# Moving the second half of the front's chunk recurrence and the samples' turn into the expert phase

## The reference, cut to what matters

```python
h = rmsnorm(x); p = h @ w_in                       # 3072 columns
y_conv = conv_mixer(...)                           # 256 channels, width 31
y_rwkv = rwkv_mixer(...)                           # 6 heads of 64: the recurrence below
y_att = sb_attention(...)                          # 6 heads; samples also read 1024 cached positions
x = x + concat(y_conv, y_rwkv, y_att) @ w_out
x = x + peer(rmsnorm(x))                           # 8 heads x 16 experts of 16384 per position

def _wkv_step(S, inp):                             # one position, every head, S is 64x64
    r, w, k, v, kk, b = inp
    sa = einsum('bhvk,bhk->bhv', S, kk)
    S = S * w[:, :, None, :] - sa[..., None] * b[:, :, None, :] + v[..., None] * k[:, :, None, :]
    return S, einsum('bhvk,bhk->bhv', S, r)
# then per head: (y - mean) * rsqrt(var + eps) * g + b, plus a bonus, times a gate
```

## Time and profile before

| | us |
|---|---|
| median of 3 runs | 3682.92 (3682.07 to 3686.68) |
| the profiled execution | 3688.43 |
| its span, first to last instruction | 3686.6 |

### The profile page before, as it was taken

The page is one execution under the profiler, slowest core; times in us unless marked ns, Lnnn a source line. Parts: engine busy times, 40 slices in busy tenths (PEclk is TensorE's granted clock), DMA queues, the critical chain, the costliest instruction groups (busy, mean ns, idle before and its releaser), DMA issues.

```text
span 3686.6 us, 52803 instructions
## 1 busy us (share of the span) xinstructions
PE 2809.8 (76%) x19164; PEld 1377.4 (37%) x19164; DVE 2585.6 (70%) x6424; ACT 1461.0 (40%) x2994; POOL 1383.0 (38%) x1205
## 2 busy tenths in 40 slices
PE   8999867667667876877688777777777777766656
PEld 4555465433224432443244334333433332323211
DVE  2477233577877787778777877788778876777775
ACT  2222112343723373338333843385338632223222
POOL 0000000144445345544454455445444555454443
PEclk9999997889888887898888888988898888778879
DMA  3112404599999999999999999999999999999998
GB/s 96 36 54 85 149 3 149 219 370 405 394 406 412 385 385 406 414 405 391 406 411 408 388 388 414 406 384 411 406 404 377 399 415 415 404 414 412 414 417 336
DMA packets 248118, 1252.97 MB, mean 340 GB/s; under 512 B 57577, under 2 KB 84497, under 8 KB 112177
## 3 DMA queue, kind: packets, MB, share of 16 engines
q0 software_dynamic: 160256, 1132.54, 76.0%
q1 hardware_dynamic: 87600, 117.05, 9.2%
HBM read 1226.61 MB, written 22.89 MB: 339 GB/s over the span
## 4 chain that ended last, share of the span: by engine, by line
PE 26%; DMA 21%; DVE 18%; ACT 10%; issue 7%; POOL 1%; another core or an unknown queue 0%; DVEq 0%; SPq 0%; ACTq 0%; POOLq 0%
PE peer_y L2289 14%; DMA uv_first<-in_peer_uv,expert 10%; DMA uv_rows<-in_peer_uv,expert 10%; PE peer_s L1977 4%; DVE uv_first L1754 4%; DVE uv_rows L1754 3%; PE scan L2082 2%; ACT L1944 2%; PE beside L2008 2%; ACT diag L1952 2%; ACT L1892 2%; DMA w_out_rows<-in_w_out 1%; DVE same L1457 1%; DVE same L1459 1%; DVE pick L1461 1%
## 5 line engine op out<-in xcount | busy, mean ns | idle before, releaser
L1413 POOL DMA_INDIRECT uv_first<-in_peer_uv,expert x604 | 706.7, 1170 | 1071.8 <-PE peer_y L2289 780.0
L2289 PE MATMUL peer_y<-uv_first,diag 64*64 64x512 f32 x4688 | 743.8, 748 | 402.4 <-ACT diag L1952 367.3
L1754 DVE CUSTOM_DVE_ANT_0 uv_first<-uv_first,p_h 128x1024 f32<-128x1024 f32 x604 | 728.4, 1223 | 198.6 <-DMA uv_first<-in_peer_uv,expert 185.9
L2289 PE MATMUL peer_y<-uv_rows,diag 64*64 64x512 f32 x3504 | 561.0, 750 | 297.8 <-ACT diag L1952 281.2
L1413 POOL DMA_INDIRECT uv_rows<-in_peer_uv,expert x452 | 533.2, 1180 | 659.5 <-PE peer_y L2289 577.0
L1754 DVE CUSTOM_DVE_ANT_0 uv_rows<-uv_rows,p_h 128x1024 f32<-128x1024 f32 x452 | 545.9, 1223 | 138.8 <-DMA uv_rows<-in_peer_uv,expert 136.8
L1944 ACT ACTIVATE gelu<-hidden 128x2 f32<-128x2 f32 x528 | 107.8, 204 | 1109.8 <-DVE hidden L1754 1054.9
L1952 ACT ACTIVATE diag<-p_ident,weights 128x128 f32<-128x128 f32 x1024 | 355.8, 395 | 478.9 <-DVE weights L1481 435.8
L2289 PEld LDWEIGHTS peer_y<-uv_first,diag 64*64 64x64 f32 x4688 | 181.7, 158 | 764.3 <-ACT diag L1952 512.4
L2289 PEld LDWEIGHTS peer_y<-uv_rows,diag 64*64 64x64 f32 x3504 | 134.9, 157 | 563.1 <-ACT diag L1952 396.2
L591 PE MATMUL proj<-mix,w_in_tile 128*128 128x512 f32 x672 | 296.9, 600 | 0.0
(11 more groups left out here) (413 smaller groups left out, 4162.4 us busy)
## 6 DMA issues: line engine op xcount, KB each, us to landing
w_out_rows<-in_w_out SPq DMA_DIRECT2D x50, 512.0 KB
w_in_tile<-in_w_in SPq DMA_DIRECT2D x24, 512.0 KB, 3.3
uv_first<-in_peer_uv,expert POOLq DMA_INDIRECT x604
uv_first<-in_w_query SPq DMA_DIRECT2D x8, 1024.0 KB, 6.7
uv_rows<-in_peer_uv,expert POOLq DMA_INDIRECT x452
pages_ring<-scratch_k_tiles SPq DMA_DIRECT2D x36, 192.0 KB
pages_ring<-out_v_new SPq DMA_DIRECT2D x36, 192.0 KB
scan_in<-scratch_scan_in SPq DMA_DIRECT2D x12, 480.0 KB
```

Of the source, the lines that this page charges most:

```text
L1413: pool.indirect_dma_start(out=uv(m, ALL, slice(0, 2 * D)), out_offset=None, in_=io["peer_uv"], in_offset=bass.IndirectOffsetOnAxis(ap=expe ...
L1754: nc.vector.tensor_tensor_reduce(out=uv(m, ALL, slice(0, D)), in0=uv(m, ALL, slice(0, D)), in1=h2[:, b % 2, :], scale=1.0, scalar=0.0, op0 ...
L2289: ins = nc.tensor.matmul(Y[r][rows[j], :], diag[rows[r], m % (2 * GP), rows[r]], uv(m, rows[r], slice(D + j * 512, D + (j + 1) * 512)), st ...
```

## The change

Only block 0's two chunks stay in `scan_rwkv` (one turn), which no longer loads the samples' state and masks. `finish_rwkv` handles block 0 alone, all three pairs in one instruction, and leaves its result in `mixed_first`; gates 1 and 2 follow the first six key products. Chunk 0 of block 1 runs in `peer`'s prelude, its steps 0 to 8 in beats 2 to 10 of block 0's attention and 9 to 15 between the parts of closing, scores and choice; the last key products move from beat 3 to beat 2, and the first output product from 3 to 4. In the expert phase block 0 holds chunk 1 of block 1 (from beat 1) and both of block 2 (from 25 and 43), with finishes from 18 and 59. Blocks 1 to 5 keep their steps. Block 6 holds the samples' turn in 26 steps from beat 35, with the state in the place of `w_out` rows, and block 7 its finish in beats 0 to 4. Finished rows stay in SBUF, in two buffers, where the closing reads them; the round by `mixed` goes. The helpers `scored`, `kept`, `chosen`, `exped` and `gated` give the same places as the lines that they replace. The diff is cut; the steps of `scan_sample` are those of the samples' turn before, cut into beats.

```diff
-FRONT = 2
+FRONT = 1
 NCH = SEQ // CH
 CPB = P // CH
+LATER = NBLK - 1 - FRONT
...
                         for slot, rows in ((2 * p, sb.kq[:, p, :]), (2 * p + 1, tile(R0 + p)), (2 * PR + p, tile(K0 + p)),
                                            (3 * PR + p, sb.bh[:, p, :]), (4 * PR + p, tile(V0 + p))):
                             sp.dma_start(io["scan_in"][:, :, slot, :].rearrange("n p c -> p n c"),
                                          rows[:, later].rearrange("p (n c) -> p n c", c=CH)).then_inc(scan_out, 16)
-                        sp.dma_start(io["finish_in"][:, :, 0, p, :].rearrange("b p n -> p b n"),
-                                     tile(p)[:, later].rearrange("p (b n) -> p b n", n=P)).then_inc(scan_out, 16)
+                        sp.dma_start(io["finish_in"][0:LATER, :, 0, p, :].rearrange("b p n -> p b n"),
+                                     tile(p)[:, FRONT * P:SEQ].rearrange("p (b n) -> p b n", n=P)).then_inc(scan_out, 16)
+                        sp.dma_start(io["finish_in"][LATER][:, 0, p, 0:CH], tile(p)[:, SEQ:SC]).then_inc(scan_out, 16)
                 if i == TILES:
                     sp.wait_ge(evicted, NT)
...
-        s0, tmask = t("state_sample", [P, PR, DB, HD]), t("seq_mask", [P, DB, HD])
-        spread, w0, values_by_seq = t("spread", [P, DB, HD]), t("w_state", [P, PR, HD]), t("values_spread", [P, DB, HD])
...
         pieces = [(0, 512), (512, 512), (1024, SC - 1024)]
         EARLY = FRONT * P
-        done = [(0, 0, EARLY), (EARLY, SEQ, SC - SEQ)]
...
+            load_queries(sp, io, sb, SLOTS + PR)
+            sp.wait_ge(V.sem, V.at("gated"))
+            sp.dma_start(io["mixed_first"], out[:, :, :]).then_inc(mix_out, 16)
             load_queries(sp, io, sb, SLOTS + PR + 1)
-            sp.wait_ge(mix_out, 16 * (PR + 1))
...
+            sp.wait_ge(mix_out, 16)
+            sp.wait_ge(g_out, 16 * 2 * PR)
...
-    scanned = lambda b: b + FRONT if b + FRONT < ATTENDED else None
+    scans = lambda b: ((1, 1, 1, 1), (2, 0, 25, 1), (2, 1, 43, 1)) if b == 0 else \
+        ((b + 2, 0, 2, 1), (b + 2, 1, 20, 1)) if b + 2 < ATTENDED else ()
+    finishes = lambda b: ((1, 18), (2, 59)) if b == 0 else ((b + 2, 36),) if b + 2 < ATTENDED else ((ATTENDED, 0),) if b == S_TURN + 1 else ()
+    S_STEPS = 26
...
+                for step in range(rate * (n - first), rate * (n - first) + rate):
+                    if step in range(16):
+                        scan(block, c, step)
+            if b == S_TURN and n - S_SCAN in range(S_STEPS):
+                scan_sample(n - S_SCAN)
+            for block, first in finishes(b):
+                if n - first in range(5):
+                    finish(block, n - first)
             if b == 0:
...
-        CLOSED = {3: range(0, 1), 5: range(1, 3), 6: range(3, 4), 8: range(4, 5)}
+        AHEAD = {1: range(24, 28), 2: range(28, 32)}
+        CLOSED = {4: range(0, 1), 5: range(1, 3), 6: range(3, 4), 8: range(4, 5)}
+        BESIDE = 2
...
-                    if b >= FRONT:
-                        sp.wait_ge(mixed_out, 16 * (b - FRONT + 1))
                     sp.dma_start(mixb[:, :, :], io["mixed"][b]).then_inc(mix_in, 16)
...
+            def scan_load_sample():
+
+                sp.wait_ge(FV.sem, FV.at("gated", LATER - 1))
+                sp.dma_start(xin[:, :, :], io["scan_in"][LATER * CPB]).then_inc(state_in, 16)
+                sp.dma_start(smask[:, :, :], io["scan_masks_sample"]).then_inc(state_in, 16)
+
...
+            scan_load(1, 0)
+            sp.dma_start(smask[:, :, :], io["scan_masks"]).then_inc(close_in, 16)
+            sp.dma_start(ident[:, :], io["ident"]).then_inc(close_in, 16)
+            sp.dma_start(gain2[:, :], io["norm2_g"]).then_inc(close_in, 16)
             begin_close(0)
+            sp.dma_start(ykept[:, 0, :, :], io["mixed_first"]).then_inc(first_in, 16)
             weights(0, 0)
             weights(0, 1)
-            sp.dma_start(gain2[:, :], io["norm2_g"]).then_inc(close_in, 16)
-            sp.dma_start(ident[:, :], io["ident"]).then_inc(close_in, 16)
...
-            sp.dma_start(smask[:, :, :], io["scan_masks"]).then_inc(const_in, 16)
...
+                        scan_load(1, 1)
+                        scan_load(1, CPB)
+                        scan_load(2, 0)
+                    elif scans(b):
+                        scan_load(b + 2, 1)
+                    if b == S_TURN:
+                        scan_load_sample()
                     for c in range(2, DC - 1):
                         weights(b + 1, c)
-                if scanned(b) is not None:
-                    scan_load(scanned(b), CPB)
-                if late_att(b) is not None:
-                    attention(late_att(b))
-                if scanned(b) is not None:
-                    sp.wait_ge(FV.sem, FV.at("gated", b))
-                    sp.dma_start(io["mixed"][scanned(b)][:, CT:CT + PR, :], ykept[:, :, :]).then_inc(mixed_out, 16)
+                if b == 0:
+                    attention(2)
+                    scan_load(2, 1)
+                    scan_load(2, CPB)
+                elif scans(b):
+                    scan_load(b + 2, CPB)
+                    if late_att(b) is not None:
+                        attention(late_att(b))
+                if b == S_TURN:
+                    sp.wait_ge(wo_used, ATTENDED * DC)
+                    sp.dma_start(s0, io["state_wkv"]).then_inc(state_in, 16)
+                    sp.wait_ge(ACT_S.sem, ACT_S.at("y"))
+                    sp.wait_ge(PE_S.sem, PE_S.at(f"out{PR - 1}"))
+                    sp.dma_start(fin[:, :, :, 0:CH], io["finish_in"][LATER][:, :, :, 0:CH]).then_inc(xin_in, 16)
+                    sp.wait_ge(DVE_S.sem, DVE_S.at(f"out{PR - 1}"))
+                    sp.dma_start(io["wkv_new_sample"], s0).then_inc(state_out, 16)
+                    sp.wait_ge(state_out, 16)
             sp.wait_ge(XV.sem, XV.at("state", chunk_at(ATTENDED - 1, CPB - 1)))
...
-                    if c == 0 and b > FRONT:
-                        act.wait_ge(mixed_out, 16 * (b - FRONT))
-                    keep_step("y", ykept[:, :, c * CH:(c + 1) * CH], r1_of(1))
+                    if c == 0:
+                        act.wait_ge(wo_used, (b - 1) * DC)
...
                     key_kept(nc, act, None, sb, Y, k)
                 attend(0, n)
+                if n >= BESIDE:
+                    scan(1, 0, n - BESIDE)
+            scan(1, 0, 9)
             close_root(0)
+            scan(1, 0, 10)
+            scan(1, 0, 11)
+            scan(1, 0, 12)
             close_turned(0)
             act.wait_ge(const_in, 16 * 9)
             keep(0)
+            scan(1, 0, 13)
             keep(1)
+            scan(1, 0, 14)
             exps(0)
+            scan(1, 0, 15)
             exps(1)
...
-                left = mixb[:, c, :] if c < DC - PA else att[:, c - (DC - PA), :]
+                if c == CT:
+                    if b:
+                        pe.wait_ge(FV.sem, FV.at("gated", b - FRONT))
+                    else:
+                        pe.wait_ge(first_in, 16)
+                recurrent = s_mixed if last(b) else ykept[:, b % 2, :, :]
+                left = mixb[:, c, :] if c < CT else recurrent[:, c - CT, :] if c < CT + PR else att[:, c - (CT + PR), :]
                 if b and c == DC - 1:
...
+                if m in range(PR):
+                    if m == 0:
+                        pe.wait_ge(state_in, 16 * 3)
+                        pe.wait_ge(FV.sem, FV.at("centre", LATER - 1))
+                        pe.wait_ge(FA.sem, FA.at("root", LATER - 1))
+                    if m == 2:
+                        kept_by_dve("spread0")
+                    for r in rows:
+                        ins = mm(RB[m % 2][r, :], kr[r, 2 * m, :], s0[r, m, :, :])
+                    PE_S.did(ins, f"in{m}")
+                if m == 4:
...
+                            ins = nc.tensor.matmul(lo(1)[r, i, q], s0[r, i, b, :], kr[r, 2 * i + 1, q], start=False, stop=True, skip_group_check=True)
+                    PE_S.did(ins, "y")
+                if m in (20, 22, 24):
+                    i = (m - 20) // 2
+                    kept_by_dve(f"spread_u{i}")
+                    if i == 1:
+                        kept_by_act("y")
+                    if i == 2:
+                        kept_by_dve("add0")
+                    for r in rows:
+                        mm(RB[i % 2][r, :], vk[r, PR + i, :], values[r, :, :], stop=False)
+                        ins = mm(RB[i % 2][r, :], bt[r, i, :], spread[r, :, :], start=False)
+                    PE_S.did(ins, f"out{i}")
+
...
 
-                k = b - FRONT
+                k, n_col = b - FRONT, CH if b == ATTENDED else P
+                by_row = lambda bank: bank[:, 0:PR * n_col].rearrange("p (i n) -> p i n", n=n_col)
                 if n == 0:
-                    pe.wait_ge(XA.sem, XA.at("y", chunk_at(b, CPB - 1)))
-                    pe.wait_ge(XV.sem, XV.at("state", chunk_at(b, CPB - 1)))
...
                 close_y(0, c)
```

(7 more changed lines are left out.)

869 lines of the change are left out of this document (480 added, 389 removed).

## The result

| | before | after |
|---|---|---|
| median of 4 runs, us | 3684.8 (3682.07 to 3696.96) | 3646.6 (3642.56 to 3655.36) |
| ratio, 95% interval | | 0.9892 (0.9869 to 0.9915) |
| profiled execution, us | 3688.4 | 3650.5 |
| its span, us | 3686.6 | 3648.7 |
| first expert gather, us | 698.65 | 609.19 |

The kernel is faster, by 31 to 48 us as the interval has it. The forecast was 3610 us in a range of 3590 to 3636, and the time lies above the range. In what follows, before is the kernel before the change and after the changed one. The profile of after says where the gain stayed: the front gave 89.5 us, 86.6 were forecast; the expert phase grew by 51.6 us, 14.1 were forecast.

A forecast was written before the change was run, and what follows sets the result against it. A front bound by chains between compute engines, then an expert phase bound by DMA transfers. Profiled 3688.4, less 86.6 for the earlier first gather, plus 14.1 in the expert phase, is 3615.9; less 5.5, 3610 us (range 3590 to 3636).

The forecast's parts named there:

- Projection, +1.9: Front, projection: longer stores on SyncE's queue delay the last w_in load; +1.9 us, bounds 0 and +3.
- Constants, turn 1, samples' turn, barrier, -98.5: Front, recurrence: fewer constant loads -3.2, turn 1 gone -34.8, samples' turn gone -61.0, a remaining barrier +0.5 us.
- Group norm's stage, 37 to 38 us: Front, group norm, gate and key products: 43.8 us shrinks to 37 to 38, so -6; bounds -9 and +1.
- Prelude, +16: Front, before the first expert gather: sixteen steps of one added chunk lengthen the 72.3 us by 16; bounds 0 and 29.
- Step 10's wait for zt: Prelude: step 10 waits for ScalarE's zt behind the closing's square and root, delaying the gain broadcast; +3 us.
- the rival with the prelude at its lone price: Prelude: the chunk costs what it takes alone, +29 us instead of 16; 3623 us in all, chance 0.12.
- Bytes, +3.1: Expert phase: net +1.2 MB of transfers costs +3.1 us at 400 GB/s; the state load lands in some 4 us.
- Block 0, +4 with bounds of 0 and +10: Expert block 0: one more chunk and finish, 12.8 us of TensorE and 6 of VectorE, lengthen it by 4 us.
- Block 6, +7 with bounds of 0 and +25: Expert block 6: the samples' turn, 38 us of TensorE over 26 beats, partly covered, lengthens it by 7 us.
- TensorE becomes the bound where work was put: Rival: blocks 0 and 6 cost their upper bounds, +25 + 10 instead of 11; 3634 us, chance 0.14.
- Its sign, TensorE over 90% busy there: Block 6, beats 35 to 60: TensorE expected over 90% busy and the transfer rate below 400 GB/s.
- The slower rival: Rival, expert phase: each of 52 new steps lengthens its beat; at 1.9 us a step 3698 us; chance 0.04.

The follow-up runs named there:

- the four edits: Changed kernel plus two chunks per expert block, y step over three beats, two beats from state product to use, recurrence steps before scores on TensorE: 3619.2 us, 0.9817.

## Why the prediction was wrong

Its base was the median of 3682.9; in the profile its misses are -2.9 us in the front and +37.5 in the expert phase, and the profiled execution stood 3.9 above the median, not 5.5.

- **Projection, +1.9: measured +4.6.** The load issues at 384.36, where 384.3 was worked out from the stores of the earlier trace rows. But the bound of 3 was wrong: TensorE idled 3.26 us instead of 0.54 for it, and some 1.7 us more came up by the stage's end; their cause is open.

```profile
381.40 2.25 SPq L228 DMA_DIRECT2D scratch_finish_in<-prc  x1
383.70 0.61 SPq L230 DMA_DIRECT2D scratch_finish_in<-prc  x1
384.36 1.24 SPq L206 DMA_DIRECT2D w_in_tile<-in_w_in  x1
```
```profile
389.69 3.10 PE L611 MATMUL proj<-w_in_tile,mix 128*128 128x384 f32 x6 [3.26 <-DMA w_in_tile<-in_w_in]
```

- **Constants, turn 1, samples' turn, barrier, -98.5: measured -99.4** (137.97 us of the earlier trace rows against 38.55). Right; VectorE's first copy comes 3.6 us earlier in the stage, where 3.2 were put.
- **Group norm's stage, 37 to 38 us: 35.6.** Right in kind, 2 us too careful.
- **Prelude, +16: +13.6.** The sum is right, its parts are partly luck. Up to the row that answers to 656.61 (558.66 in after) +2 was put and 5.1 measured, from there to the end of the closing products +10 and 3.6, behind them +5.4 and 4.8 (the three add up to 17.4; 16 was taken). So the closing products end 8.7 us later after the prelude's begin, where 10 to 14 were named. Step 10's wait for zt behind square and root was there, longer than thought (4.45 us at 582.52). The gather at 609.2 lies in the stated 600 to 622; the rival with the prelude at its lone price is out.
- **Bytes, +3.1.** The state load issued at 3016.87 us and landed 8.7 us later, twice the 4 that were worked out, but still inside its three beats. By the run without the turn's compute, block 6 keeps 4 us and block 7 3 for the turn's bytes and its finish, and blocks 1 to 5 hold 5 to 6 us together that no experiment touched; that may be bytes or chance. Blocks 1 to 5 each stayed within 4 us, two of them outside the 3 that I had named, about the scatter. (In the earlier trace rows the sixth slice is at 0 and the eighth at 5, not full as I wrote; nothing in the sum hangs on it.)
- **Block 0, +4 with bounds of 0 and +10: +12 to +21.** The failed step. It compared averages, "12.8 us of TensorE, 6 of VectorE, on 244 and 274 busy of 352". The room that counts is what VectorE waits for gathers: 30 us over the block in the kernel before, but 4.9 in beats 45 to 60, where attention 2 runs and where the chunk was put. And the chunk takes from it not its 4 us of VectorE alone, but also its waits for TensorE (6.2 us). The sum also put nothing for the start of block 1's second chunk in beat 1, behind the third scores (a wait of 6.4 us); by beat 9 block 0 is 5 to 7 us behind.
- **Block 6, +7 with bounds of 0 and +25: +25.** The second failed step. The size lies at the upper bound, but not for the bound's reason. The step weighed TensorE's load, "107 + 38 = 145 of 144 us". That load never came: TensorE's busy time in beats 35 to 63 rose from 115.4 to 134.8 us of 178.8, as the granted clock rose from 0.78 to 0.83, and with the four edits to 126.7 of 155.5 us, with no loss in that stretch. The step named one heavy step (10.5 us; 7.9 in after) and left out VectorE, which gets 16.1 us of work there and 31.7 us of waits for TensorE, 47.8 us. Its waits for gathers, 34.2 us, went down to 7.7 and gave 26.5 of that; with 2.0 us of waits for gelu and other gaps the stretch is 23.3 us longer.
- **The rivals.** "TensorE becomes the bound where work was put", 3634 us, came nearest in time and place, and its mechanism is refuted by the runs with two beats from product to use, with steps ahead of the scores and with the four edits: the same matmuls, 14, 7 and 16 us less in block 6 (12, 5 and 15 with block 7). Its sign, TensorE over 90% busy there, didn't come either: 75%. The slower rival had the right loop, but its uniform price is refuted by the run with two chunks in every block. What I called for it, POOL's wait on peer_y, doesn't tell waits of the loop from those of full rings; VectorE's waits do.

The 96 small matmuls of beat 53 took 7.9 us, 82 ns each, after 109 in the earlier trace rows. The difference is the clock: in after they start 56 ns apart up to 3148.4 us, at a granted clock of 0.99, and 104 ns apart from 3149.9 us on, at 0.50; in the earlier trace rows the granted clock is 0.56. The Trainium skill ("TensorE: Matmul & The Clock Gate", section "Wait — 56ns, not 53.3ns?") has 25 ns as the least distance of two small matmuls; neither row comes near it, and the rows were rightly preferred, though the sum hardly hung on it: without them, block 6 lost 2.5 us less.

The 5 to 7 us of beats 0 to 9 in block 0 are placed (a step behind the scores) but not settled in size. With two beats from product to use, block 6 is still 11 us behind before, 8.9 of them in beats 35 to 63; there they went only with the three other edits in place, so the y step's share is not shown apart.

## What to carry to other kernels

When work is put beside a saturated transfer, don't compare its length with an engine's idle share of a stage. Read from the stretch itself how long the engine that consumes the transfers waits for them; in the two stretches read here that was the most that could be taken, and the added work draws on it with its busy time on that engine and with every wait for another engine that it brings into that engine's order. A step that is handed to another engine and read back one beat later makes a serial round with everything queued ahead of it there: leave two beats, keep it out of beats with a long item ahead of it, or put it ahead of that item. Where the consumer still waits for transfers, as in the kernel before, such a round cost nothing that could be measured.

## What the runs showed of the hardware

A wait that closes such a round also slows what is in it: the 16 expert matmuls took 1.95 us at 3163.8 (in the run without the small matmuls and in after) and 3.69 us at 3170.4, after 3.94 us without work for TensorE; the granted clock of after from 3170 to 3175 us is 0.50, the lower level. The sum for block 6 had no term for this.

Idle time is not the only thing that came ahead of the lower level. In after TensorE is busy without a gap from 3145.28 to 3153.36 us with the y step, most of it the 96 small matmuls (64x4), and its granted clock falls from 0.99 to 0.50 meanwhile; the 16 expert matmuls right behind it, at 3154.73, took 3.69 us too.
